# Down stages of three feed-forwards: a Strassen scheme on eight of the 22 tiles, the halves of the output in turn

## The reference, cut to what matters

```
def swiglu(x, wg, wu, wd):
    return (jax.nn.silu(x @ wg) * (x @ wu)) @ wd        # wg, wu: 1024 x 2816, wd: 2816 x 1024

for l in range(2):
    x = x + 0.5 * swiglu(rmsnorm(x, ffn1_norm[l]), ffn1_wg[l], ffn1_wu[l], ffn1_wd[l])
    x = x + mixer(rmsnorm(x, mix_norm[l]))
    x = x + 0.5 * swiglu(rmsnorm(x, ffn2_norm[l]), ffn2_wg[l], ffn2_wu[l], ffn2_wd[l])
return rmsnorm(x, final_norm)
```

## Time and profile before

| | us |
|---|---|
| median of 3 executions | 1879.25 (1879.05 to 1879.32) |
| profiled execution, its own time | 1878.08 |
| its span in the trace | 1876.3 |
| TensorE busy in the span | 1848.7 (99%) |
| VectorE busy | 1303.7 (69%) |
| ScalarE busy | 919.5 (49%) |
| GpSimd busy | 222.8 (12%) |

### The profile page before, as it was taken

How to read it: one execution, slowest core, us unless ns; L and a number is a source line. 1 busy time by engine, 2 the same in 40 slices (tenths; PEclk the granted TensorE clock), 3 DMA queues, 4 the chain that set the end, 5 groups by cost and what they waited for, 6 DMA issues and landing times.

```text
span 1876.3 us, 31626 instructions
## 1 busy us (share of the span) xinstructions
PE 1848.7 (99%) x11410; PEld 1629.9 (87%) x11410; DVE 1303.7 (69%) x1921; ACT 919.5 (49%) x1589; POOL 222.8 (12%) x205
## 2 busy tenths in 40 slices
PE   8999999999999999999999999999999999999998
PEld 7899988878888889998888999888777888999887
DVE  7899843667656679983367999525896677899434
ACT  4555532427556445552344555323487543555323
POOL 0100000210233210000021000001256221000002
PEclk9999999999999999999999999999999999999999
DMA  5233333222211223233222233322321022332331
GB/s 174 82 107 112 115 109 111 83 90 55 93 46 46 96 84 113 92 132 113 89 90 90 90 115 109 134 89 90 103 90 46 23 70 88 113 112 105 119 108 60
DMA packets 36718, 177.72 MB, mean 95 GB/s; under 512 B 12560, under 2 KB 14096, under 8 KB 16160
## 3 DMA queue, kind: packets, MB, share of 16 engines
q1 hardware_dynamic: 34496, 173.24, 27.0%
q10 hardware_dynamic: 1952, 2.85, 0.5%
q0 software_dynamic: 192, 0.59, 0.1%
HBM read 174.56 MB, written 2.10 MB: 94 GB/s over the span
## 4 chain that ended last, share of the span: by engine, by line
PE 90%; DVE 6%; ACT 2%; issue 1%; DMA 1%; POOL 0%; ACTq 0%; POOLq 0%; DVEq 0%
PE ps L373 29%; PE ps L375 28%; PE ps L374 28%; PE ps L1716 1%; DVE wl L301 1%; PE ps L1248 1%; PE ps L1320 1%; DMA raw<-in_units 1%; PE ps L1738 1%; ACT wh L297 1%; DVE ws L626 1%; DVE wl L608 0%; PE ps L1447 0%; PE ps L1310 0%; PE ps L1230 0%
## 5 line engine op out<-in xcount | busy, mean ns | idle before, releaser
L301 DVE TENSOR_TENSOR wl<-raw,wh 128x2048 fp32r<-128x2048 f32 (+1 forms) x92 | 213.4, 2319 | 336.7 <-ACT wh L297 336.5
L373 PE MATMUL ps<-tmh,wh 128*128 128x256 f32 (+1 forms) x1344 | 407.8, 303 | 0.0
L374 PE MATMUL ps<-tml,wh 128*128 128x256 f32 (+1 forms) x1344 | 407.5, 303 | 0.0
L375 PE MATMUL ps<-tmh,wl 128*128 128x256 f32 (+1 forms) x1344 | 407.3, 303 | 0.0
L373 PE MATMUL ps<-xgh,wh 128*128 128x512 f32 (+1 forms) x960 | 350.1, 365 | 5.5 <-DVE xgl L426 3.1
L375 PE MATMUL ps<-xgh,wl 128*128 128x512 f32 (+1 forms) x960 | 344.8, 359 | 0.0
L374 PE MATMUL ps<-xgl,wh 128*128 128x512 f32 (+1 forms) x960 | 344.8, 359 | 0.0
L297 ACT ACTIVATE wh<-raw 128x2048 fp32r<-128x2048 f32 (+1 forms) x92 | 174.6, 1898 | 344.0 <-PE ps L375 343.9
L374 PEld LDWEIGHTS ps<-tml,wh 128*128 128x128 f32 x1344 | 252.5, 188 | 12.6
L373 PEld LDWEIGHTS ps<-tmh,wh 128*128 128x128 f32 x1344 | 252.5, 188 | 12.4
L375 PEld LDWEIGHTS ps<-tmh,wl 128*128 128x128 f32 x1344 | 252.4, 188 | 12.4
(11 more groups left out here) (334 smaller groups left out, 3368.3 us busy)
## 6 DMA issues: line engine op xcount, KB each, us to landing
raw<-in_units SPq DMA_DIRECT2D x160, 1024.0 KB, 4.9
out<-xg SPq DMA_DIRECT2D x4, 512.0 KB, 2.6
relb<-in_rpb SPq DMA_DIRECT2D x64, 24.0 KB, 2.1
x<-in_xT ACTq DMA_DIRECT2D x2, 512.0 KB, 7.0
x<-in_xT SPq DMA_DIRECT2D x2, 512.0 KB, 7.6
raw<-in_units SPq DMA_DIRECT2D x2, 256.0 KB, 5.5
raw<-in_units ACTq DMA_DIRECT2D x2, 256.0 KB, 9.6
xg<-in_last_gain ACTq DMA_DIRECT2D x1, 512.0 KB, 3.8
```

Source lines behind the costliest of these rows:

```text
L301: nc.vector.tensor_tensor(wl[:, c % 2, 0:n], raw[:, c % 2, 0:n], wh[:, c % 2, 0:n].bitcast(F32), ALU.subtract).then_inc(w_lo, 1)
L373: nc.tensor.matmul(dst, lh, rh, start=first, stop=False, skip_group_check=onto)
L374: nc.tensor.matmul(dst, lh, rl, start=False, stop=False, skip_group_check=onto)
L375: return nc.tensor.matmul(dst, ll, rh, start=False, stop=last, skip_group_check=onto)
```

## The change

It concerns f = 0, 1 and 2 alone; the last feed-forward keeps its down stage.

- The product with `wd` is split over its 22 input tiles. Tiles 0 to 7 go through a Strassen scheme, in two pairs of units, one for output blocks 0 to 3 and one for 4 to 7, each 14 products of 4 x 3 matmuls of 256 columns. Tiles 8 to 21 stay plain, with 512 columns.
- The output is made in two halves (`phases_pe`): three plain units for blocks 0 to 3, the first Strassen pair, one unit with tiles 20 and 21 for all eight blocks, two plain units for blocks 4 to 7, the second Strassen pair, one plain unit for blocks 4 to 7. Still eleven units of weights, reordered on the host (`down_units`).
- The activations need a Strassen form too: three quadrants of 128x1024 split (`d_quad_hi`, `d_quad_lo`), four sums of quadrants on VectorE (`d_right_sum`) and their split (`d_sums_hi`, `d_sums_lo`). Tiles 8 to 19 are split twice, once for each half (`two_hi`, `two_lo`, p = 0 to 12, two tiles each).
- The products that go to one output quadrant are added in its bank. Those that are shared are evacuated: `d_copy_act` copies three partial sums of 256 columns for each of two blocks to `mc`, `d_shared_dve` and `d_chain_dve` add them to `x`.
- Output blocks 0 to 3 are finished after the first half; `finish_act` and `finish_dve` do the rest at the end.
- The loops of these down stages are written out.
- TensorE waits for all 26 tile splits of a feed-forward before the last unit.

```diff
@@ prods_act @@
-                    if r_next is None:
+                    if r_next is None and f < 3:
+                        two_hi(act, f, c_down, 0)
+                    elif r_next is None:
                         a_hi_act(act, f, 0)
@@ new functions @@
+        def two_hi(act, f, c, p):
+            for k2 in range(2):
+                if p < 7:
+                    act.wait_ge(a32_done, 22 * f + two_tile(f, p) + k2 + 1)
+                if k2 == 0 and p == 1:
+                    act.wait_ge(w_half, 2 * c)
+                if k2 == 0 and p >= 2 and p != 7 and p != 8:
+                    act.wait_ge(w_half, two_free(c, p))
...
+                nc.scalar.activation(two_part(p, k2)[0], a32[:, two_tile(f, p) + k2, :], ACT.Copy).then_inc(a_hi, 1)
+        def two_lo(dve, f, p):
+            for k2 in range(2):
+                dve.wait_ge(a_hi, 26 * f + 2 * p + k2 + 1)
+                h, l = two_part(p, k2)
+                nc.vector.tensor_tensor(l, a32[:, two_tile(f, p) + k2, :], h.bitcast(F32), ALU.subtract).then_inc(a_lo, 1)
+        def half_unit_pe(pe, f, c, i, p0, k, b0, first, last):
+            s = (c + i) % 2
+            for p in (p0, p0 + 1):
+                pe.wait_ge(a_lo, 26 * f + 2 * p + 2)
+                for k2 in range(2):
+                    for b in range(4):
+                        o = ((p - p0) * 2 + k2) * 512 + b * P
+                        mm = three(ps[:, b0 + b, :], wh[:, s, o:o + P], wl[:, s, o:o + P], *two_part(p, k2),
+                                   first and p == p0 and k2 == 0, False)
+                mm.then_inc(w_half, 1)
+        def phases_pe(pe, f, c, n):
+            pe.wait_ge(s_comb, d_base_comb(f) - 4)
+            for i in range(3):
+                pe.wait_ge(w_lo, c + i + 1)
+                half_unit_pe(pe, f, c, i, 2 * i, 4, 0, i == 0, False)
+            pe.wait_ge(s_comb, d_base_comb(f))
+            for j in range(N_STEP):
+                d_prod_pe(pe, f, c + 3, 0, j)
+            pe.wait_ge(w_lo, c + 6)
+            pe.wait_ge(a_lo, 26 * f + 14)
+            s = (c + 5) % 2
+            for b in range(KD):
+                if b == 4:
+                    pe.wait_ge(s_copy, d_base_copy(f) + 6)
+                    pe.wait_ge(s_comb, d_base_comb(f) + 8)
...
+            for i, p0 in ((6, 7), (7, 9)):
+                pe.wait_ge(w_lo, c + i + 1)
+                half_unit_pe(pe, f, c, i, p0, 4, 4, False, False)
+            pe.wait_ge(x_new, 8 * n + 4)
+            for j in range(N_STEP):
+                d_prod_pe(pe, f, c + 8, 1, j)
+            pe.wait_ge(w_lo, c + 11)
+            pe.wait_ge(a_lo, 26 * (f + 1))
...
+        def phases_dve(dve, f, c, n):
+            two_lo(dve, f, 1)
+            split_lo(dve, c + 1)
+            d_quad_lo(dve, f, 0)
+            d_quad_lo(dve, f, 1)
+            two_lo(dve, f, 2)
+            d_quad_lo(dve, f, 2)
+            for i in range(2):
+                d_right_sum(dve, f, i)
+            two_lo(dve, f, 3)
+            for i in range(2, 4):
+                d_right_sum(dve, f, i)
+            split_lo(dve, c + 2)
+            two_lo(dve, f, 4)
+            for i in range(2):
+                d_sums_lo(dve, f, i)
+            for i in range(4):
+                d_left_sum(dve, f, c + 3, 0, 0, i)
+            two_lo(dve, f, 5)
+            for i in range(2, 4):
+                d_sums_lo(dve, f, i)
+            for j in range(5):
+                d_left_lo(dve, f, c + 3, 0, j)
+            d_pair_dve(dve, f, 0, c + 3, c + 5, 6)
+            two_lo(dve, f, 7)
+            two_lo(dve, f, 8)
+            split_lo(dve, c + 6)
+            dve.wait_ge(s_comb, d_base_comb(f) + 8)
+            for b in range(4):
+                dve.wait_ge(y_done, 7 * n + b + 1)
+                nc.vector.scalar_tensor_tensor(x[:, b, :], ps[:, b, :], 0.5, x[:, b, :],
+                                               ALU.mult, ALU.add).then_inc(x_new, 1)
+            for b in range(4):
+                lo_x(dve, n + 1, b)
+            split_lo(dve, c + 7)
+            for i in range(4):
+                d_left_sum(dve, f, c + 8, 1, 0, i)
+            two_lo(dve, f, 9)
+            two_lo(dve, f, 10)
+            for j in range(5):
+                d_left_lo(dve, f, c + 8, 1, j)
+            d_pair_dve(dve, f, 1, c + 8, c + 10, 11)
+            two_lo(dve, f, 12)
+            split_lo(dve, c + PAIRS)
+            dve.wait_ge(s_comb, d_base_comb(f) + 16)
+            finish_dve(dve, n + 1, 0.5, c + PAIRS - 1, b0=4)
+        def d_pair_dve(dve, f, h, S, c_next, p_next):
+            for j in range(N_STEP):
+                if j in (5, 12):
+                    d_shared_dve(dve, f, S, h, j // 12)
+                if j in (6, 13):
+                    d_chain_dve(dve, f, h, j // 13)
+                if j < 4:
+                    d_left_sum(dve, f, S, h, 1, j)
+                if j + 5 < N_STEP:
+                    d_left_lo(dve, f, S, h, j + 5)
+                if j == 9:
+                    two_lo(dve, f, p_next)
+                if j == 11:
+                    split_lo(dve, c_next)
```

More of the change, by code:

```diff
@@ L404, in block_T2, with finish_dve @@
                     mm.then_inc(xg_free, 1)
[L406 to L409 removed]
+        def finish_dve(dve, n, scale, last_unit, held=KD, split=None, b0=0):
+            for b in range(b0, KD):
                 if b == KD // 2 and split is not None:
@@ L427, in lo_x, with finish_act @@
                                            xgh[:, b, :].bitcast(F32), ALU.mult, ALU.subtract).then_inc(xg_lo, 1)
-        def finish_act(act, n, last_unit=None, held=KD, split=None):
-            for b in range(KD):
+        def finish_act(act, n, last_unit=None, held=KD, split=None, blocks=range(KD)):
+            for b in blocks:
                 if b == KD // 2 and split is not None:
@@ new lines, in d_bank, with d_prod_pe @@
+        def d_bank(h, x_, a):
+            m = 4 * h + 2 * x_
+            spare = 4 - 4 * h + x_
+            bank, half = {A11: (spare, 0), S2: (spare, 0), S1: (spare, 0), S3: (spare + 2, 0),
+                          A12: (m, 0), S4: (m, 1), A22: (m + 1, 0)}[a]
+            return ps[:, bank, half * HALF:(half + 1) * HALF]
+        def d_prod_pe(pe, f, S, h, j):
+            x_, a, b = STEPS[j]
+            copies = d_base_copy(f) + 6 * h + 3 * x_
+            if a == A22:
+                pe.wait_ge(w_lo, S + x_ + 1)
+            else:
+                pe.wait_ge(s_lo, d_left_count(f, h, j))
+            if a == S2:
+                pe.wait_ge(s_copy, copies + 1)
+            if a == S1:
+                pe.wait_ge(s_copy, copies + 2)
+            lh, ll = slot(wh, S, j), slot(wl, S, j)
+            for k in range(4):
+                mm = three(d_bank(h, x_, a), lh[:, k * P:(k + 1) * P], ll[:, k * P:(k + 1) * P], *d_right(b, k),
+                           k == 0 and a in (A11, S3), k == 3 and a in (A11, S2, S1, S3), a in (S2, S1))
+            mm.then_inc(*((w_half, 2) if j in (10, 13) else (s_prod, 1)))
@@ L939, in ffn_pe @@
             c = B + 2 * PAIRS
+            if not last:
+                phases_pe(pe, f, c, n)
+                return
             down_pe(pe, f, c, 0)
@@ L979, in ffn_act @@
                 setup_act(act)
+            if not last:
+                phases_act(act, f, c, n)
+                return
             with act.Fori(0, (PAIRS - 1) // 2) as j:
@@ L983, in ffn_act @@
                     a_hi_act(act, f, t, j)
[L984 to L989, removed]
+            final_act(act)
         def ffn_dve(dve, f, B, n, last):
@@ L1041, in ffn_dve @@
                 setup_dve(dve)
+            if not last:
+                phases_dve(dve, f, c, n)
+                return
             with dve.Fori(0, (PAIRS - 1) // 2) as j:
@@ L1045, in ffn_dve @@
                     a_lo_dve(dve, f, t, j)
[L1046 to L1051, removed]
+            final_dve(dve, c + PAIRS - 1)
         def ffn_pool(pool, f, B, n):
```

245 lines of the change are left out of this document (219 added, 26 removed).

## The result

The changed kernel takes 1889.40 us (median of 5, 1887.37 to 1889.69) against 1879.32 us of the kernel before (5, 1879.05 to 1879.34): ratio 1.0055, 95% interval 1.0044 to 1.0066. It is slower by 10.1 us, where the prediction had +2.3 and "within 0.2%" as the likeliest, and the time lies above the range.

What follows compares the result with a forecast made beforehand. TensorE, busy 99% of the span, was taken as the bound. Saving 15.2 us and adding 2.4, 11.7 and 3.4 gave +2.3, a median of 1881.5 us, range 1873.5 to 1887.5.

Steps and rivals of the forecast that it cites:

- The count of work: Down stages: 336 matmuls of 256 columns replace 192 of 512, saving 5.06 us a stage, 15.2 us in three.
- The estimate of +7.8 us a stage: Down stages: at 98 ns per 256-column and 131 ns per 512-column matmul, the change would cost 7.8 us; given no chance.
- The turn before unit 5: Behind the first Strassen pair of each changed down stage: TensorE waits for the unit split, 0.81 us, 2.4 in three.
- The turn before the last unit: Behind the second pair: TensorE waits for VectorE's last tile split, 3.90 us with the first matmul, 11.7 in three.
- VectorE in the first units: Start of down stages: no cost in f = 1 and 2; the setup chain makes f = 0 lose 3.4 us, once.
- The sum: Whole kernel: -15.2 + 2.4 + 11.7 + 3.4 = +2.3 us; stages f = 1 and 2 shorter by 0.3, f = 0 longer by 3.
- The step that failed: Gap before each last unit: 3.6 us idle is shorter than the 3.9 to 4.4 for a clock fall; no cost.
- the rival's bare centre: Clock falls in the gap before each last unit: three times 2 is +6 us, 1887.5; chance 0.12.

Runs made afterwards that it cites:

- e9_halfs: Changed kernel, tiles 18 and 19 split earlier, setup chain moved, unit behind each Strassen pair split in halves, first after product 8: 1861.50 us beside 1878.03.
- e10_bhalfs: Kernel before, plain down stages, with the unit split in two halves at its four turns from up to down stage: 1875.03 us, ratio 0.9983.
- e1_fill: Changed kernel plus 15 unread matmuls of 512 columns on TensorE ahead of its wait before each changed down stage's last unit: 1882.54 us beside 1877.77.
- e2_mid: Changed kernel with VectorE's split of tiles 18 and 19 put ahead of the four adds of the second block pair: 1881.22 us beside 1877.77.
- e8_hold: Kernel before, plain down stages, with six idle VectorE additions that TensorE waits for before the last unit in f = 0, 1, 2: 1895.80 us beside 1878.03.
- e5_both: Changed kernel with tiles 18 and 19 split beside 16 and 17, and the f = 0 setup chain moved before the second pair: 1869.85 us beside 1878.03.
- e3_early: Changed kernel with ScalarE's and VectorE's split of tiles 18 and 19 put beside that of tiles 16 and 17: 1874.34 us beside 1877.77.

## Why the prediction was wrong

**The count of work** was right: 1008 narrow matmuls more, 576 wide ones fewer, at 0.1144 and 0.2265 us; the stages of e9_halfs and e10_bhalfs confirm the saving to 0.3 us a stage. The estimate of +7.8 us a stage, worked out in the prediction from the sustained distances of the Trainium skill, has no support: the stage with the scheme is the shorter one.

**The turn before unit 5** (0.81 forecast): 0.80 from start to start, as in the old place. (The turn from the up stage, which the prediction left at its old length, has 0.85 in the changed kernel.)

**The turn before the last unit** (3.79, released by VectorE): 3.96 from start to start less the 0.11 slot is 3.85. Right in size, place, cause and order of the queue. It could be read off before anything ran, because each of the six operations behind which TensorE waits had its distance in the old trace.

**VectorE in the first units**: no wait of TensorE in f = 1 and 2 there, as forecast; VectorE's distances on the quadrants are 1.13 to 1.20. In f = 0 one gap of 2.39 with 2.8 forecast, and in all 3.3 us (123.96 against 120.65 in e1_fill) with 3.4 forecast.

**The sum** of these steps was -0.35, -0.35 and +3.0 us for the stages. With the clock held up (e1_fill) they are +0.03, +0.04 and +3.34. So the schedule was forecast to 1.1 us in three stages, and most of that is the saving: 4.75 us a stage between e9_halfs and e10_bhalfs, not 5.06. The start of the kernel added about 0.5, which the prediction did not have: in the kernels of the new form the first matmul after the start comes at 8.9 to 9.3 us, in the plain ones at 8.2 to 8.4. Its cause was not tried.

**The step that failed** is the one on the clock, the term that the sum put at nothing: "Against: 3.6 is shorter than 3.9". I took one row, the fall in the empty tail of the kernel, 3.9 to 4.4 us after the last matmul, for the point from which it decides. It is no such point. In the changed kernel the clock fell in all three gaps of 3.69 us, in f = 0 and 2 about when TensorE resumed, in f = 1 two and a half us after the last matmul; in e2_mid it fell behind 1.82 us, and in e8_hold two of three gaps passed, each 3.96 us from start to start like those of the changed kernel. The one gap that spoke for safety, 2.51 us at the start, was one draw of several. At this very place the clock fell in four of the 13 profiled executions (e2_mid, e3_early, e5_both, e9_halfs), behind 2.09 to 2.71 us, and it stayed up in the changed kernel behind 3.30. Two lines each, of e5_both and of the changed kernel:

```profile
9.21 0.47 PE L376 MATMUL ps<-xgh,wh 128*128 128x512 f32 x1 [2.09 <-DVE xgl L429]
10.20:13.00 2.80, 2.80 (x8) 2.17 (x7) 2.03 (x3) 1.97 (x5) 0.00 (x0) 0.50 1.07 411
...
9.13 0.47 PE L376 MATMUL ps<-xgh,wh 128*128 128x512 f32 x1 [3.30 <-DVE xgl L429]
9.00:12.00 3.00, 2.87 (x13) 2.41 (x14) 2.37 (x4) 1.86 (x3) 0.00 (x0) 1.00 1.08 400
```

The mechanism and its price of 2 us a stage were in the text, and the price was near (1.60, 2.46, 1.49 in the profile, 5.3 for all three on the times of e1_fill). Its chance of 0.12 was far too low, and the range ended at the rival's bare centre, 1887.5. With a fall in every gap the sum would have been 1881.5 + 6 = 1887.5 as the likeliest, clearly slower, and the range would have reached beyond it.

The Trainium skill, "TensorE: Matmul & The Clock Gate", section "Part 1", which I had named behind that rival, says that an idle array drops to half clock until it has been busy again. The trace of the changed kernel agrees: 0.50 behind the three gaps and 1.00 once the last unit had run for 3 to 6 us. The gaps of e8_hold that passed show that not every idle stretch of this length does it. The rule should have moved the chance, not just stood behind it.

**The size of the whole**: the profiled execution is 9.3 us over that of the kernel before (1887.37 against 1878.08): 5.6 for the clock, 3.4 for the stages without it and 0.4 ahead of the first stage, which make 9.4. The medians are 10.1 apart, 0.8 more; the slower executions of the changed kernel have the lower mean clock (0.993 against 0.995), but no trace shows where they lost it.

## What to carry to other kernels

What a scheme saves, here 4.75 us of a stage of 120, is easily eaten by one wait at one of its seams, here 3.96 us from start to start and a fall of the clock behind it: put the preparation for the step behind a seam ahead of the evacuation of the step before it, and count what stands in the one queue between. Count a gap of TensorE of some 2 us or more, in a kernel that is otherwise dense, at its own length and with a chance of a fall of the clock on top, some 1.5 to 2.5 us here. Whether it falls differed between traces in the same place, so a mean over a few executions is needed, and one trace without a fall proves nothing. To part the two costs, fill the gap with matmuls that nobody reads.

## What was not expected of the hardware

- The granted clock fell to 0.50 for gaps of TensorE as short as 1.82 us (e2_mid, f = 2), while two of about twice that length, 3.57 us, passed (e8_hold, f = 1 and 2). The fall can also come after TensorE is at work again: in f = 0 of the changed kernel TensorE resumes at 345.01, and the clock is 1.00 from 345.0 to 345.3 and 0.50 from 345.5.
- At the lower level 512 columns take 0.43 us from start to start and not 0.2265, so a fall costs about half of the time that TensorE works at that level: in f = 1 of the changed kernel from 961.3 to about 966.6, 5.3 us, for a loss of 2.46.
- The same gap in the same place differs between traces: 1.82 to 1.87 us of idle time in the second mixer with a fall in three of 13, and the gap at the start with a fall in four of 13.
- A single execution can hide it: the profiled execution of e8_hold has one fall in three gaps, and is 4.1 to 5.5 us under the other three.
